# The last chunk of the down product: its seven block products in another order, and the mean and eps of the final norm inside the square root

## The reference

```python
    hf = _rmsnorm(x, g_ffn)
    x = x + (jax.nn.silu(hf @ w_ffn_gate) * (hf @ w_ffn_up)) @ w_ffn_down
...
def _rmsnorm(x, g):
    xf = x.astype(jnp.float32)
    y = xf * lax.rsqrt(jnp.mean(xf * xf, axis=-1, keepdims=True) + RMS_EPS)
    return (y * g.astype(jnp.float32)).astype(x.dtype)
...
    y_prompt = _rmsnorm(xp, g_final)
    y_sample = _rmsnorm(xs, g_final)
```

## Time and profile before

| | us |
|---|---|
| three runs: median, lowest, highest | 1928.87, 1927.39, 1930.49 |
| the profiled execution, its own time | 1929.79 |
| its span, first to last instruction | 1928.1 |

### The profile page before, as it was taken

The page is one execution under the profiler, slowest core; times in us unless marked ns, Lnnn a source line. Parts: engine busy times, 40 slices in busy tenths (PEclk is TensorE's granted clock), DMA queues, the critical chain, the costliest instruction groups (busy, mean ns, idle before and its releaser), DMA issues.

```text
span 1928.1 us, 33351 instructions
## 1 busy us (share of the span) xinstructions
PE 1861.6 (97%) x12769; PEld 1700.6 (88%) x12769; DVE 1198.3 (62%) x2357; ACT 711.6 (37%) x1302; POOL 879.5 (46%) x694
## 2 busy tenths in 40 slices
PE   6899999999999999999999999799999999999996
PEld 6699999989988888888799988699999999977885
DVE  5699997344555423566765514866676566666568
ACT  5533222232333454655743203423333233323233
POOL 3342223332322340101024112768788778778877
PEclk9999999999999999999999999799999999999998
DMA  5132332222221362454744242122232222646422
GB/s 174 36 91 84 124 100 90 89 90 67 78 84 51 96 192 102 157 183 162 268 152 128 76 156 88 53 83 88 100 126 99 83 83 88 240 156 219 137 76 92
DMA packets 167749, 223.66 MB, mean 116 GB/s; under 512 B 11368, under 2 KB 122766, under 8 KB 167086
## 3 DMA queue, kind: packets, MB, share of 16 engines
q1 hardware_dynamic: 161614, 202.77, 31.3%
q0 software_dynamic: 5984, 18.82, 2.9%
HBM read 152.34 MB, written 68.92 MB: 115 GB/s over the span
## 4 chain that ended last, share of the span: by engine, by line
PE 42%; DVE 3%; issue 2%; POOL 2%; DMA 2%; ACT 1%; SPq 0%; DVEq 0%; ACTq 0%; POOLq 0%
PE lgt L1570 4%; PE lgt L1573 4%; PE lgt L1572 4%; PE ring L1127 4%; PE ring L1129 4%; PE ring L1128 4%; PE ring L1570 3%; PE ring L1573 3%; PE ring L1572 3%; PE lgt L1607 2%; PE lgt L1609 1%; PE lgt L1611 1%; PE ring L1607 1%; PE ring L1609 1%; PE ring L1611 1%
## 5 line engine op out<-in xcount | busy, mean ns | idle before, releaser
L1127 PE MATMUL ring<-n_hi,piece_hi 128*128 128x352 f32 (+1 forms) x1312 | 434.8, 331 | 1.6 <-ACT arena L1650 0.9
L1129 PE MATMUL ring<-n_hi,piece_lo 128*128 128x352 f32 (+1 forms) x1312 | 422.9, 322 | 0.0
L1128 PE MATMUL ring<-n_lo,piece_hi 128*128 128x352 f32 (+1 forms) x1312 | 422.1, 322 | 0.0
L3085 POOL TENSOR_TENSOR piece_lo<-piece_whole,piece_hi 128x1024 fp32r<-128x1024 f32 (+2 forms) x48 | 105.8, 2205 | 502.2 <-ACT piece_hi L1663 502.0
L1650 ACT ACTIVATE arena<-ring 128x352 f32<-128x352 f32 (+6 forms) x359 | 148.1, 436 | 390.6 <-PE ring L1129 289.6
L3256 POOL TENSOR_TENSOR weight_lo<-weight_raw,weight_hi 128x512 fp32r<-128x512 f32 x154 | 228.2, 1502 | 109.8 <-ACT weight_hi L2056 108.5
L1127 PEld LDWEIGHTS ring<-n_hi,piece_hi 128*128 128x128 f32 (+1 forms) x1312 | 246.6, 188 | 9.0 <-issue 6.6
L1128 PEld LDWEIGHTS ring<-n_lo,piece_hi 128*128 128x128 f32 (+1 forms) x1312 | 247.3, 188 | 0.4
L1129 PEld LDWEIGHTS ring<-n_hi,piece_lo 128*128 128x128 f32 (+1 forms) x1312 | 246.2, 188 | 0.3
L2360 DVE TENSOR_SCALAR_CACHE_REDUCE arena<-arena 128x384 uint8<-128x384 f32 (+6 forms) x224 | 190.6, 874 | 1.4 <-DVE arena L2360 0.2
L1570 PE MATMUL lgt<-s_hi,weight_hi 128*128 128x264 f32 x528 | 152.2, 288 | 10.0 <-ACT part_e L2121 7.7
(11 more groups left out here) (390 smaller groups left out, 4514.9 us busy)
## 6 DMA issues: line engine op xcount, KB each, us to landing
piece_whole<-w_in SPq DMA_DIRECT2D x54, 512.0 KB, 3.7
projected_rows<-arena SPq DMA_DIRECT2D x44, 528.0 KB, 2.7
rows_raw<-ffn_rows SPq DMA_DIRECT2D x21, 768.0 KB, 5.2
arena<-projected_rows SPq DMA_DIRECT2D x12, 1056.0 KB, 6.0
weight_raw<-w_ffn_gate SPq DMA_DIRECT2D x11, 1024.0 KB, 5.5
weight_raw<-w_ffn_up SPq DMA_DIRECT2D x11, 1024.0 KB, 7.7
down_raw<-w_ffn_down SPq DMA_DIRECT2D x3, 3072.0 KB, 10.7
arena<-projected_rows SPq DMA_DIRECT2D x16, 528.0 KB, 3.7
```

The lines of the kernel that those rows point to most:

```text
L1127: pe.matmul(out, lhi, rhi, start=first, stop=False)
L1128: pe.matmul(out, lhi, rlo, start=False, stop=False)
L1129: return pe.matmul(out, llo, rhi, start=False, stop=last)
L3085: ins = g.tensor_tensor(lo, raw, hi, ALU.subtract)
```

## The change

1. In the last chunk, and in it alone, the products come as S1, S4, S2, P11, P12, S3, P22 (`ORDER`). The bank groups follow (`GROUPS`), and the numbers of a product in the loads, splits, waits and counts are looked up by its turn (`turn_of`, `group_of`).
2. In the last chunk the first weight difference goes to a buffer of its own (`t1_last`), since P11 still has to read the block; GpSimd's order is written out by hand. `v_sum` is complete with P11, the fourth product; its additions to the low rows' left halves (`add_v`) stand on VectorE behind P11's blocks 1 to 3 and P12's first, those to the top rows' right halves on GpSimd ahead of the last split.
3. The square of a top row now also waits for P12's addition. In the final norm, ScalarE takes the root of (sum of squares)/D + eps in one instruction, with a scale and an eps column (`eps_row`); `out_mean` is gone.
4. `out_rows(0)` is still behind (S4, 3); the sample rows' additions are behind S1; the other `out_rows` are placed anew.

```diff
+        ORDER = [[P11, P12, PS1, PS4, PS2, PS3, P22]] * LASTQ + [[PS1, PS4, PS2, P11, P12, PS3, P22]]
+        GROUPS = [[(P11, P12), (PS1, PS4), (PS2,), (PS3, P22)]] * LASTQ + [[(PS1, PS4), (PS2,), (P11, P12), (PS3, P22)]]
+        TURN = [(q, j) for q in range(len(KCS)) for j in ORDER[q]]
...
+        def turn_of(q, j):
+
+            return STEPS * q + ORDER[q].index(j)
...
+        def raw_block(q, j):
+
+            return t1_last if (q, j) == (LASTQ, PS1) else dwr[q % 2][col_block(j, KCS[q])]
...
                 elif i < 4:
                     act.wait_ge(x_sum_pool, i + 1)
+                    act.wait_ge(dn_used, dn_count(LASTQ, P12, i))
...
-                act.wait_ge(y_ms, NT + n + 1)
-                act.activation(rt[0:r, i:i + 1], msq[0:r, i:i + 1], ACT.Sqrt).then_inc(y_rt, 1)
+                act.wait_ge(act_seq, seq[0])
+                act.activation(rt[0:r, i:i + 1], ssq[0:r, i:i + 1], ACT.Sqrt, scale=1.0 / D, bias=eps_row[0:r, :])\
+                   .then_inc(y_rt, 1)
...
             link(v.memset(one, 1.0))
+            link(v.memset(eps_row, EPS))
...
+            def add_v(t):
+
+                v.wait_ge(dn_used, dn_count(LASTQ, P11, t))
+                part = low_x[:, t, 0:512]
+                v.tensor_tensor(part, part, v2[:, t, :], ALU.add).then_inc(x_sum_dve, 1)
+
             def end_rows(j, t):
 
-                if (j, t) == (PS4, 0):
-                    out_mean(0)
-                elif (j, t) == (PS4, 3):
+                if (j, t) == (PS4, 3):
                     v.wait_ge(x_landed[1], 64)
                     out_rows(0)
-                elif j == PS3 and t >= 1:
-                    out_mean(t)
+                elif j == P11 and t >= 1:
+                    add_v(t - 1)
+                elif j == P12:
+                    if t == 0:
+                        add_v(3)
                     if t >= 2:
                         out_rows(t - 1)
-                elif j == P22:
-                    if t == 0:
-                        out_mean(4)
-                    if t <= 1:
-                        out_rows(3 + t)
-                    else:
-                        out_mean(3 + t)
-                        if t == 3:
-                            out_rows(5)
+                elif j == PS3 and t <= 1:
+                    out_rows(3 + t)
+                elif (j, t) == (P22, 2):
+                    out_rows(5)
...
-                    if q == LASTQ and j == P11:
+                    if q == LASTQ and j == PS1:
                         v.wait_ge(smp_full, len(KCS))
...
+            down_sum(LASTQ, 0)
+            down_lo(LASTQ, PS1)
+            down_lo(LASTQ, PS4)
+            down_sum(LASTQ, 1)
+            down_sum(LASTQ, 2)
+            down_lo(LASTQ, PS2)
+            down_lo(LASTQ, P11)
+            down_lo(LASTQ, P12)
+            down_sum(LASTQ, 3)
+            down_lo(LASTQ, PS3)
             for t in range(4):
-                g.wait_ge(dn_used, dn_count(LASTQ, PS2, t))
+                g.wait_ge(dn_used, dn_count(LASTQ, P11, t))
                 part = top_x[:, t, 512:1024]
                 g.tensor_tensor(part, part, v2[:, t, :], ALU.add).then_inc(x_sum_pool, 1)
+            down_lo(LASTQ, P22)
```

More of the change, by code:

```diff
@@ L591, in build @@
         hw = placed("h2_rows", F32, base, KD, T)
+        eps_row = tiny(1)
         gain = placed("gains", F32, small + 403, KD)
@@ L640, in build @@
         v2 = placed("v_sum", F32, base, 4, 512)
+        t1_last = placed("down_sum1", F32, o_a1 + 5 * D, KCS[LASTQ], 512)
+        assert 5 * D + KCS[LASTQ] * 512 <= 4 * W4
         xsmp = placed("x_sample", F32, o_a1 + 5 * W4, D)
@@ L788, in ff_count, with group_of @@
             return 4 * STEPS * p + 4 * j + n + 1
+        def turn_of(q, j):
+            return STEPS * q + ORDER[q].index(j)
+        def group_of(q, j):
+            return 4 * q + [j in g_ for g_ in GROUPS[q]].index(True)
         def dn_count(q, j, t):
-            return 4 * STEPS * q + 4 * j + t + 1
+            return 4 * turn_of(q, j) + t + 1
         def col_block(j, kc):
@@ L1015, in load_rows @@
             def load_rows(k):
-                q, j = k // STEPS, k % STEPS
+                q, j = TURN[k]
                 last_p = MK * q + KCS[q]
-                if j == P11:
+                if k % STEPS == 0:
                     sp.wait_ge(act_out[0], 32 * last_p)
@@ L1588, in down_block @@
             def down_block(q, j, t):
-                k = STEPS * q + j
-                s_ = 16 * q + 4 * {P11: 0, P12: 0, PS1: 1, PS4: 1, PS2: 2, PS3: 3, P22: 3}[j] + t
+                k = turn_of(q, j)
+                s_ = 4 * group_of(q, j) + t
                 first = j in (P11, PS1, PS2, PS3)
                 if not first:
-                    pe.wait_ge(dn_used, dn_count(q, j - 1, t))
+                    pe.wait_ge(dn_used, dn_count(q, {P12: P11, PS4: PS1, P22: PS3}[j], t))
                 elif s_ < 3:
@@ L1599, in down_block @@
                     old = s_ - 7
-                    oq, oj, ot = old // 16, (P12, PS4, PS2, P22)[old % 16 // 4], old % 4
+                    oq, oj, ot = old // 16, GROUPS[old // 16][old % 16 // 4][-1], old % 4
                     pe.wait_ge(dn_used, dn_count(oq, oj, ot))
@@ L1626, in _ @@
             for q in range(len(KCS)):
-                for j in range(STEPS):
-                    k = STEPS * q + j
+                for j in ORDER[q]:
+                    k = turn_of(q, j)
                     pe.wait_ge(w_lo_done, W_PARTS + k + 1)
@@ L2123, in down_hi @@
             def down_hi(q, j):
-                k, kc = STEPS * q + j, KCS[q]
+                k, kc = turn_of(q, j), KCS[q]
                 if k >= 3:
@@ L2197, in _ @@
             for k in range(2, STEPS * len(KCS) - 1):
-                down_hi(k // STEPS, k % STEPS)
+                down_hi(*TURN[k])
             def out_squares(n):
@@ L2945, in row_lo @@
             def row_lo(k):
-                kc = KCS[k // STEPS]
+                kc = KCS[TURN[k][0]]
                 v.wait_ge(comb_hi_done, H_PARTS + k + 1)
@@ L2998, in add_down @@
                     if q > 0 or j in (PS2, PS3):
-                        v.wait_ge(dn_used, dn_count(q, j, t) - 8)
+                        v.wait_ge(dn_used, dn_count(q, j, t) - (4 if (q, j) == (LASTQ, P11) else 8))
                     if q == LASTQ and j == P22:
@@ L3003, in add_down @@
                 ins.then_inc(dn_used, 1)
[L3005 to L3010, removed]
             def out_rows(n):
@@ L3068, in _ @@
                         ins.then_inc(x_sum_dve, 1)
-            out_mean(7)
             out_rows(6)
-            out_mean(8)
             out_rows(7)
@@ L3285, in down_lo @@
             def down_lo(q, j):
-                k, kc = STEPS * q + j, KCS[q]
+                k, kc = turn_of(q, j), KCS[q]
                 g.wait_ge(w_hi_done, W_PARTS + k + 1)
-                whole = dwr[q % 2][col_block(j, kc)]
+                whole = raw_block(q, j)
                 for kk in range(kc):
@@ L3298, in down_sum @@
                                       for ks in range(2) for ds in range(2))
-                if n == 0:
+                t1 = t1_last if q == LASTQ else b11
+                if n == 0 and q == LASTQ:
+                    g.wait_ge(dwr_landed[q % 2], 16 * (q // 2 + 1))
+                    g.wait_ge(w_lo_done, W_PARTS + STEPS * LASTQ)
+                elif n == 0:
                     g.wait_ge(smp_full, q + 1)
@@ L3302, in down_sum @@
                 elif n == 1:
+                    g.wait_ge(smp_full, q + 1)
                     g.wait_ge(w_t_done, W_SUMS + 4 * q + 1)
                 elif n == 2:
-                    g.wait_ge(w_lo_done, W_PARTS + STEPS * q + PS4 + 1)
+                    g.wait_ge(w_lo_done, W_PARTS + turn_of(q, PS4) + 1)
                 else:
+                    g.wait_ge(w_lo_done, W_PARTS + turn_of(q, P12) + 1)
                     g.wait_ge(w_t_done, W_SUMS + 4 * q + 3)
-                whole, less, out = ((b12, b11, b11), (b22, b12, b12), (b22, b11, b22), (b21, b22, b21))[n]
+                whole, less, out = ((b12, b11, t1), (b22, b12, b12), (b22, t1, b22), (b21, b22, b21))[n]
                 for kk in range(kc):
@@ L3342, in _ @@
                     weight_sum(p + 1, 1)
-            for k in range(2, STEPS * len(KCS)):
-                q, j = k // STEPS, k % STEPS
+            for k in range(2, STEPS * LASTQ):
+                q, j = TURN[k]
                 down_lo(q, j)
```

6 lines of the change are left out of this document (3 added, 3 removed).

## The result

The changed kernel is slower by **0.26%**: the ratio of its time to that of the kernel before, run beside it, is 1.0026, with a 95% interval of 1.0016 to 1.0036. On 1930 us that is 5.0 us, from 3.1 to 6.9; the forecast was 4.9.

A forecast was written before the change was run, and what follows sets the result against it. VectorE was taken to bound the tail. The walks of both orders differ by 4.2 us, the clock adds 0.7: 4.9 us slower, 1933.8 us as a median (1934.7 profiled), range 1929.8 to 1938.

The forecast's parts named there:

- Nothing for the sums, the splits' move and the memset: Last chunk's sums and splits, and the start's eps memset: no cost, as TensorE's queued products and a DMA wait cover them.
- The hold of 9 us: VectorE at out_rows(0) behind S4: reached by 1884.1, stands until ScalarE's root is over at 1893.07, 9 us.
- TensorE's gaps: New TensorE idle times in the tail: 2.8 and 2.2 us near 1892 to 1898, 2.8 at about 1910, two of 1.5.
- VectorE's own work, 30.3 us: VectorE from 1893.07: 20 PSUM additions, 3 splits, 4 sum additions, 9 output tiles; 30.3 us, to 1923.4 without a wait.
- The meetings with GpSimd, 4.8 us: Tail: VectorE's two-SBUF-input instructions wait out GpSimd's: sum additions, last split and two y, 4.8 us, to 1928.2.
- a shared bandwidth: Alternative to the exclusive hold of the VectorE-GpSimd SBUF pair: both slow whenever they overlap, some 8 us instead of 4.8.
- The clock, 0 to 1.6 us: Gaps drop TensorE to 1.2 GHz; P22's last two blocks at 2.7 us delay VectorE by 0 to 1.6, taken 0.7.
- the square of tile 4: ScalarE's square of that tile in the tail has its input ready late: another 0.4 us, to 1928.6.
- The mean in the root: Final norm: nine VectorE means of 0.07 us go (0.6); last four tile cycles fall from 1.51 to 1.39; root takes 0.20.
- rival D: out_rows(0) finds its root ready, as ScalarE reaches the sample square earlier: 1.3 us less, 1927.6; chance 0.05.
- B: VectorE catches up in the tail: losses to SBUF access and late squares under 4.8 us; say 1930.5; chance 0.12.
- C: TensorE's clock stays low from P12 on, blocks of 2.7 us: 12 us more, 1941; chance 0.07, around 1938.

The follow-up runs named there:

- run 2: Changed kernel with out_rows(0) moved behind the fourth block of P11, the fourth product; tail 52.2 us, ratio 1.0003 to the kernel before.
- run 3: Changed kernel with ScalarE's sample-row square and root taken ahead of the split for P12, out_rows(0) left behind S4; tail 50.8 us, ratio 0.9991.
- (7): Changed kernel with out_rows(0) behind S2's fourth block, one product later; VectorE stands 4.15 us, tail 54.4 us, ratio 1.0012.
- run 1: Kernel before, old order and means, with out_mean(0) and out_rows(0) behind the fourth block of the second product, P12; tail 61.5 us, ratio 1.0051.
- Run 5: Changed kernel with GpSimd's eight additions of the common sum cut from 512 columns to 8, results incomplete; tail 53.2 us, ratio 1.0003.
- (6): Changed kernel with matmuls that nobody reads put into TensorE's new gaps; tail 58.0 us, ratio 1.0032.
- run 4: Kernel before in its old order, with only the mean and eps put inside the root; tail 51.0 us, ratio 0.9990.
- run 8: Run 3's early square, plus v_sum's fourth addition and the y of tiles 3 and 4 placed later on VectorE; tail 48.0 us, ratio 0.9983.

## Why the prediction was right

**The size.** 4.9 us forecast, 5.0 measured by ratio, 6.2 in the profiled tail, all inside the range. That 4.9 and 5.0 agree so closely is in part luck, as the interval goes from 3.1 to 6.9. By the tail the sum is 1.3 short: 1.0 of that is in the meetings with GpSimd, and 0.2 in the moment at which VectorE goes on (1893.07 forecast; 1890.74 with the 2.5 us that this execution was ahead is 1893.26). Some of the signs came out just beyond their bounds for that: on the same axis, the last y ends at 1930.5 (forecast 1928 to 1930) and the last matmul at 1925.0 (1921 to 1924), and the third product's first addition starts at 1894.7 (after 1895). The steps, in the prediction's order:

- *Nothing for the sums, the splits' move and the memset: right in the rows.* The first three products of the last chunk run without a gap in the changed kernel, and TensorE's first idle time there is the one ahead of P11's fourth block.
- *The hold of 9 us: right.* 9.16 us. Undone in two ways (runs 2 and 3), halved (7) and made alone (1), it accounts for the 6.2 us: 58.4 to 52.2, or to 50.8 where the output isn't moved into the crowded part.
- *TensorE's gaps: four of the five came, one of them at half its size.* 2.8, 2.2, 2.8 and two of 1.5 were forecast; there are 2.91, 1.08, 3.06 and 1.26, and before the third block of P22 TensorE had just come free. The second is shorter since the fourth block of P11, at the low clock, fills it.
- *VectorE's own work, 30.3 us: right.* From the first reciprocal at 1890.74 to 1927.97 it is 37.23; less what it waited for GpSimd (5.8) and its idle 0.98, 30.4.
- *The meetings with GpSimd, 4.8 us (its parts add up to 4.7): right in kind, a microsecond short.* By the durations above 0.67, 1.20 and 1.28: the first three additions of the sum 1.6, the split 1.0, the fourth addition 1.1, two y 2.1, together 5.8. The split is the term that was mis-sized most, 0.4 for 1.04; the three additions were 0.4 short in all. Run 5 shows that GpSimd's additions are what most of these instructions wait for. From 1893.87 on, the kernel before loses 5.1 us in the same way (the y of the sample rows 0.7, a split 1.0, three additions 1.5, four y 1.9), so this is a price of both orders, and no more than 0.7 of the loss is in it. The Trainium skill (SBUF — State Buffer, Who interferes with whom) calls the port pair that VectorE and GpSimd share an exclusive lock, held for the whole instruction; the rows agree with that, since the addition of 0.67 grew to at most 1.77 and the y of 1.28 to 2.35, by less than one GpSimd instruction of 1.27. The forecast for a shared bandwidth was 8 us, and 5.8 is nearer to the lock's 4.8.
- *The clock, 0 to 1.6 us, taken at 0.7, beside 0.4 for the square of tile 4: right in kind, a little high in size.* The prediction counts the prompt tiles from 0 here, so its tiles 2, 3 and 4 are tiles 3, 4 and 5 elsewhere in this text. The two came as one, 0.98 us, because they overlap: taking the clock away (6) brings the square's 0.45 back. The clock alone is worth 0.4 to 0.5.
- *The mean in the root: right.* 1.2 us by run 4, where the sum of its parts in rival D was 1.3. The root itself takes 0.29 to 0.30 in place of the 0.20 that I took, so ScalarE needs 1.45 a tile. That costs nothing there, as the last four y of run 4 stay 1.39 apart; in the changed kernel the last three do, and P22's last addition stands ahead of them.

**The rivals.** B (VectorE catches up) needed losses under 4.8 us behind the hold; they were 5.8 + 0.98. C (low clock throughout) didn't come: the clock was back at 1.00 by 1902. D (no hold) is what run 3 makes of the kernel, 1.4 us less than before where D said 1.3, but its price was too good for the other way of undoing the hold: with `out_rows(0)` moved (run 2) the tail is 52.2, not 51. I had not priced the output in its new place, where it is 2.24 us of an engine that is full to the end.

## What to carry to other kernels

When products, tiles or stages are put in another order, an instruction that is tied to a stage's name moves with it, while what it waits for may be tied to a count on another engine. For each such instruction, ask when it is now reached and when its input is made; a 1.4 us output that VectorE reached 9 us too early cost 6 us here, because twenty additions from PSUM and three splits were queued behind it. An engine that bounds the tail makes up only a part of idle time that it has ahead of the tail: 3 of 9 us here, and nothing in run 1, where TensorE had no work that it could do meanwhile.

## What the runs showed of the hardware that I had not expected

- A 128x1 square root with a scale and a bias column took 0.29 to 0.30 us on ScalarE, the one without 0.20.
- After an idle time of TensorE of 2.91 us, one block of work and another idle time of 1.08, the granted clock was 0.50 to 0.56 from 1893 to 1899, and 1.00 again from 1902 on. VectorE's work hid that.
- A y of a 128x1024 tile, 1.28 us otherwise, took 1.44 to 2.35 us beside GpSimd's work. In run 8, against run 3, another order of the same instructions on VectorE took 1.6 us off four of them.
